# Router tail and first expert pass of a hybrid decoder layer: a second signal for the selection copy, a root split between two engines, and another order of membership and logits

## The reference, cut to what matters

```
x = x + einsum('bsc,cd->bsd', mixed, w_out)              # output projection
h = rms_norm(x, norm_ffn_g)
g_prob   = softmax(h @ w_rg + b_rg);  g_top, g_idx = top_k(g_prob, 1)     # 4 groups
e_logits = (h @ w_re + b_re)[group g_idx]                                # 8 experts in each
e_prob   = softmax(e_logits);  e_top, e_idx = top_k(e_prob, 2)
combine  = one_hot(g_idx*8 + e_idx) * (e_top / sum(e_top) * g_top)
act = silu(h @ w_gate[e]) * (h @ w_up[e]) * combine[e]     # 32 experts, 256 wide
x = x + sum_e act @ w_down[e]
return rms_norm(x, norm_final_g)
```

## Time and profile before

| | |
|---|---|
| median of 3 runs | 364.67 us (364.49 to 366.02) |
| the profiled execution | 363.79 us, of which its span is 361.6 us |
| PE busy | 312.5 us, 86% |
| DVE busy | 163.9 us, 45% |
| ACT busy | 125.0 us, 35% |
| POOL busy | 42.7 us, 12% |
| DMA | 121.17 MB, mean 335 GB/s |

### The profile page before, as it was taken

How to read it: one execution, slowest core, us unless ns; L and a number is a source line. 1 busy time by engine, 2 the same in 40 slices (tenths; PEclk the granted TensorE clock), 3 DMA queues, 4 the chain that set the end, 5 groups by cost and what they waited for, 6 DMA issues and landing times.

```text
span 361.6 us, 11575 instructions
## 1 busy us (share of the span) xinstructions
PE 312.5 (86%) x4740; PEld 240.3 (66%) x4741; DVE 163.9 (45%) x453; ACT 125.0 (35%) x307; POOL 42.7 (12%) x73
## 2 busy tenths in 40 slices
PE   1799999999999989889979898889999999766571
PEld 1699989889875545667657665657677777546250
DVE  2635545383353612774535344435555544341334
ACT  4726336545241426533313232312323323220223
POOL 1200000363402225620000000000000000000002
PEclk9899999999999999999989999999999999998997
DMA  8999795062729989489999999999999999999943
GB/s 254 352 386 387 263 392 239 3 237 112 280 81 400 314 353 387 160 304 348 418 414 357 418 418 414 416 418 410 423 412 421 418 415 423 410 424 416 414 175 116
DMA packets 32652, 121.17 MB, mean 335 GB/s; under 512 B 5497, under 2 KB 7825, under 8 KB 24689
## 3 DMA queue, kind: packets, MB, share of 16 engines
q1 hardware_dynamic: 32480, 120.65, 85.1%
q10 hardware_dynamic: 144, 0.13, 0.1%
HBM read 119.72 MB, written 1.05 MB: 334 GB/s over the span
## 4 chain that ended last, share of the span: by engine, by line
PE 68%; issue 8%; DMA 7%; DVE 4%; DVEq 4%; SPq 4%; ACT 3%; POOL 0%; POOLq 0%; ACTq 0%
PE bank L494 13%; PE bank L770 8%; PE bank L738 7%; PE bank L698 7%; PE bank L561 7%; PE bank L488 7%; DMA spare<-in_w_up_dram 6%; PE bank L705 4%; SPq L360 2%; PE bank L508 2%; PE bank L759 2%; ACT yb L1016 2%; PE bank L523 1%; DVEq L1431 1%; DMA ring<-in_norm_ffn_g_dram 1%
## 5 line engine op out<-in xcount | busy, mean ns | idle before, releaser
L738 PE MATMUL bank<-ring,hT 128*32 128x128 f32 x1664 | 53.2, 279 | 12.7 <-issue 4.7
L738 PEld LDWEIGHTS bank<-ring,hT 128*32 128x32 f32 x1664 | 46.1, 112 | 23.8 <-issue 23.3
L1426 DVE SCALAR_TENSOR_TENSOR yb<-bank,pp,yb 64x512 fp32r<-64x512 f32 x36 | 27.0, 749 | 45.8 <-ACT yb L1016 45.2
L1173 DVE TENSOR_TENSOR unit_lo<-ring,unit_hi 128x2048 fp32r<-128x2048 f32 (+1 forms) x12 | 26.3, 2207 | 32.6 <-ACT unit_hi L839 32.6
L698 PE MATMUL bank<-pp,qk 128*128 128x64 bf16 x912 | 30.6, 194 | 8.2 <-issue 4.7
L698 PEld LDWEIGHTS bank<-pp,qk 128*128 128x128 bf16 x912 | 28.1, 98 | 13.4 <-issue 7.4
L1016 ACT ACTIVATE yb<-bank,pp 64x512 fp32r<-64x512 f32 x36 | 24.6, 683 | 28.9 <-PE bank L770 28.4
L1078 POOL TENSOR_TENSOR stats<-stats 128x1 f32<-128x1 f32 (+1 forms) x7 | 4.6, 664 | 219.8 <-DVE stats L1457 199.7
L561 PE MATMUL bank<-ring,qk 128*128 128x512 f32 (+1 forms) x72 | 29.9, 551 | 0.0
L770 PE MATMUL bank<-ring,pp 128*32 128x512 f32 x208 | 25.0, 598 | 0.0
L705 PE MATMUL bank<-yb,selT 128*128 128x512 f32 x76 | 23.3, 428 | 1.7 <-DVE yb L1426 1.6
(11 more groups left out here) (197 smaller groups left out, 513.6 us busy)
## 6 DMA issues: line engine op xcount, KB each, us to landing
ring<-in_w_up_dram SPq DMA_DIRECT2D x24, 1024.0 KB, 19.1
ring<-in_w_down_dram SPq DMA_DIRECT2D x24, 1024.0 KB, 19.1
ring<-in_w_gate_dram SPq DMA_DIRECT2D x22, 1024.0 KB, 16.9
ring<-in_w_in_dram SPq DMA_DIRECT2D x5, 2048.0 KB, 19.4
ring<-in_w_out_dram SPq DMA_DIRECT2D x4, 1024.0 KB, 8.5
spare<-in_w_gate_dram SPq DMA_DIRECT2D x4, 1024.0 KB, 19.0
spare<-in_w_up_dram SPq DMA_DIRECT2D x4, 1024.0 KB, 19.7
work<-in_w_gate_dram SPq DMA_DIRECT2D x4, 1024.0 KB, 16.8
```

The source lines that it names most:

```text
L738: last = mm(p_gu[b:b + CAP, w * P:(w + 1) * P], hg[:, k, CAP * e:CAP * (e + 1)], w_gu[at[e]][:, w, k, h, :], start=(k == 0), stop=(k == KD ...
L1173: V.tensor_tensor(unit_lo[b][:, k, :], unit_src(u)[:, k, :], unit_hi[b][:, k, :].bitcast(fp32), ALU.subtract).then_inc(w_lo_ready, 1)
L1426: V.scalar_tensor_tensor(out=yb[half][rest, :], in0=p_y[rows, :], scalar=wcol[rows, :], in1=yb[half][rows, :].bitcast(fp32), op0=ALU.mult, ...
```

## The change

Five edits, all in the router's tail and in the signals of a pass:

1. PE: the four logit products of chunk 1 stood ahead of the last output projection. They now stand behind it, two ahead of the last chunk's transposes and two behind them, and `router_logits(3)` is behind those too.
2. DVE: `members(0)` stood right behind `best_two(0)`. It now stands behind the copy of chunk 3, the second tile's `mean_square` and the last `add_projection`.
3. ACT squares with a scale of 1/32, so its sums are already divided by 1024. `mean_square` is one DVE instruction in place of two for either tile. For tile 1 it adds the first two of three sums and no longer waits for the last chunk's.
4. POOL: `last_power` adds the last chunk's sum and then raises to -0.5, in place of `power(5, ...)`.
5. DVE makes the selection copy in `copy_selection` with a semaphore of its own, `selo_ready`; ahead of the first pass it stands ahead of the two `gain` instructions. PE waits for `selo_ready` ahead of the root products and for `selw_ready` only ahead of the transposed selection.

```diff
@@ tensor
+            def router_logits(n, k0=0, k1=KD):
-                for k in blocks(n):
+                for k in blocks(n)[k0:k1]:
...
             router_logits(2)
-            router_logits(1)
             out_proj(G_OM + LAST, 0, 2)
             transpose_x(3)
             out_proj(G_OM + LAST, 2, 4)
+            router_logits(1, 0, 2)
+            transpose_x(LAST)
+            router_logits(1, 2, 4)
             router_logits(3)
-            transpose_x(LAST)
             router_logits(LAST)
...
                         pe.wait_ge(selT_ready, i + 1)
-                        pe.wait_ge(selw_ready, i + 1)
+                        pe.wait_ge(selo_ready, i + 1)
                         for t in range(NT):
                             picked = mm(p_tr[:, 3 * P + 1:3 * P + 4], selo[:, t, :], rst[:, t, :], start=(t == 0), stop=(t == NT - 1))
...
                 pe.wait_ge(rrow_ready, i + 1)
+                pe.wait_ge(selw_ready, i + 1)
                 for t in range(NT):
                     mm(p_tr[:, t * P:(t + 1) * P], selo[:, t, :], identb, start=True, stop=True)
@@ scalar
-                ins = A(rest_of[n], x_chunk(n), ACT.Square, accum_out=sq5[:, SQ_AT[n]:SQ_AT[n] + 1])
-                if n in (2, LAST):
+                ins = A(rest_of[n], x_chunk(n), ACT.Square, scale=D ** -0.5, accum_out=sq5[:, SQ_AT[n]:SQ_AT[n] + 1])
+                if n >= 2:
                     ins.then_inc(ssq_ready, 1)
@@ gpsimd
+            def last_power():
+                pool.wait_ge(var_ready, 6)
+                pool.wait_ge(ssq_ready, 5)
+                step(nc.gpsimd.tensor_tensor(var[:, 1:2], var[:, 1:2], sq5[:, 4:5], ALU.add))
+                nc.gpsimd.tensor_tensor(rstdf[:, 1:2], var[:, 1:2], mhalf[:, 1:2], ALU.pow).then_inc(pow_ready, 1)
...
-            power(5, rstdf, 1, 1)
+            last_power()
@@ vector
                 dve.wait_ge(ssq_ready, 3 + t)
-                if t == 0:
-                    step(V.tensor_tensor(var[:, c], sq5[:, 0:1], sq5[:, 1:2], ALU.add))
-                else:
-                    step(V.scalar_tensor_tensor(out=var[:, c], in0=sq5[:, 2:3], scalar=sq5[:, 3:4], in1=sq5[:, 4:5],
-                                                op0=ALU.add, op1=ALU.add))
-                V.tensor_scalar(var[:, c], var[:, c], 1.0 / D, EPS, ALU.mult, ALU.add).then_inc(var_ready, 1)
+                V.tensor_scalar(var[:, c], sq5[:, 2 * t:2 * t + 1], sq5[:, 2 * t + 1:2 * t + 2], EPS, ALU.add, ALU.add).then_inc(var_ready, 1)
...
             best_two(0)
+            take_xT(3)
+            mean_square(1)
+            add_projection(G_OM + LAST)
             members(0)
-            take_xT(3)
-            add_projection(G_OM + LAST)
             take_xT(LAST)
-            mean_square(1)
...
+            def copy_selection(passes_before):
+                dve.wait_ge(sel_ready, passes_before + 1)
+                V.tensor_copy(selo.rearrange("p t (h c) -> p t h c", h=2),
+                              selb.unsqueeze(2).to_broadcast([P, NT, 2, CP])).then_inc(selo_ready, 1)
...
+            copy_selection(0)
             dve.wait_ge(gathered_half, 1)
             gain(0, p_hg).then_inc(hg_half_ready, 1)
...
-            weigh(0, 0)
+            weigh(0)
...
                 dve.wait_ge(actt_done, i + 1)
-                weigh(at_next, i + 1)
+                copy_selection(i + 1)
+                weigh(at_next)
```

More of the change, by code:

```diff
@@ L290, in layer_program @@
         r1_dve_ready, lo_dve_ready = sem("r1_dve_ready"), sem("lo_dve_ready")
-        hg_half_ready, gathered_half = sem("hg_half_ready"), sem("gathered_half")
+        hg_half_ready, gathered_half, selo_ready = sem("hg_half_ready"), sem("gathered_half"), sem("selo_ready")
         gate_half_done, gate_done = sem("gate_half_done"), sem("gate_done")
@@ L643, in transpose_x @@
                 last.then_inc(x2t_done, 1)
-            def router_logits(n):
+            def router_logits(n, k0=0, k1=KD):
                 t = CHUNKS[n][0]
@@ L1387, in _, with weigh @@
             step(V.tensor_tensor(wgt[:, :, 0:E], chosen[:, :, 0], chosen[:, :, 1], ALU.add))
-            def weigh(at_e, passes_before):
-                dve.wait_ge(sel_ready, passes_before + 1)
-                V.tensor_copy(selo.rearrange("p t (h c) -> p t h c", h=2), selb.unsqueeze(2).to_broadcast([P, NT, 2, CP]))
+            def weigh(at_e):
                 for t in range(NT):
@@ L1453, in _ @@
             own(2)
-            dve.wait_ge(ssq_ready, 5)
+            dve.wait_ge(ssq_ready, 6)
             V.tensor_tensor(ssq, ssq4[:, :, 0], ssq4[:, :, 1], ALU.add).then_inc(dve_step, 1)
```

## The result

| | before | after |
|---|---|---|
| median of 12 runs | 364.23 us (362.77 to 366.02) | 362.12 us (359.95 to 366.44) |
| profiled execution, its span | 363.79, 361.6 us | 362.38, 360.4 us |
| last up weights landed | 343.72 | 340.98 |
| from there to the end | 17.9 us | 19.4 us |

The ratio is 0.9941 (95% interval 0.9917 to 0.9965): 2.1 us faster, where 1.4 was forecast (363.3 us). In the profiled pair the span is 1.2 us shorter.

A forecast was written before the change was run, and what follows sets the result against it. The unbroken weight stream bounds the kernel, fed by PE's progress up to 193 us. Router's tail 1.1 plus first pass 0.3 gives 1.4 us, so 363.3 us against the median of 364.67; range 361.8 to 365.2.

The forecast's parts named there:

- What bounds: Whole kernel: time is the unbroken weight stream's start, plus its bytes at 417 GB/s, plus 17.9 us.
- Router's tail: From the last add to expert 6's down weights: ranks, selection, gather and those weights come 1.1 us earlier, bounds 0.4 to 1.3.
- Between transposes and `start_acc`: PE in the router's tail: six products plus transposes not overlapped take 1.6 us, where 1.40 us passed before.
- the power: POOL, last chunk's root: starts about 151.3 behind a 0.20 us addition, takes 0.84 us, ends 152.15.
- The membership: DVE, router's tail: moving `members(0)` from ahead of chunk 3's copy lets the last add start at 149.9 instead of 150.96.
- Copy beside POOL not stretched: DVE's copy of chunk 3 stays at 0.41 us beside POOL; if stretched, 1.1 us and a gain of 0.4.
- Move of PE's products: PE's logit products behind the last output projection: buys DVE almost nothing, expert 5's gate weights are issued at 149.0.
- First pass: Root products lose a 0.93 us wait, but the gather starts only 0.3 us earlier; bounds 0 to 0.93.
- Rival A: Third pass's 2.42 us PE stall changes; without it the 192 to 195 hole vanishes, 1.3 us more, 362.0 us; chance 0.16.
- the hole at 192 to 195: DMA falls to 232 GB/s, waiting for PE's fourth pass; lacks 1.3 us of transfers, forecast to get 0.3 shorter.
- The tail of 17.9 us: From the last up weights' landing to the end (last pass, final norm, stores): 17.9 us, untouched by the change.
- the forecast's own signs of being wrong: Stall near 182 of another length, chunk 3's copy over 0.5 us, or last weights not moving as PE did at 193.

The follow-up runs named there:

- experiment 4: Changed kernel with `members(0)` back right behind `best_two(0)`, ahead of the copy of chunk 3: 367.80 us, ratio 1.0094 to the kernel before.
- experiment 9: Changed kernel, equal instruction count, four 512-column products replacing the last k-block of up products in couples 5, 9 and 13: 363.48 us, ratio 0.9972 to the kernel before.
- experiment 12: Changed kernel without the scaled squares, shorter mean square and `last_power`: 363.79 us, ratio 0.9996 to the kernel before.
- experiment 11: Changed kernel with `members(0)` in its old place and two 512-column identity products ahead of the last transposes: 363.71 us, ratio 0.9989 to the kernel before.
- experiment 3: Changed kernel with PE's old order of logit products and last transposes: 363.25 us, ratio 0.9969 to the kernel before.
- experiment 1: Kernel before plus only the selection copy's own signal `selo_ready`: 364.99 us, ratio 1.0019 to the kernel before.
- experiment 2: Changed kernel without the selection copy's own signal, the router edits staying: 362.77 us, ratio 0.9966 to the kernel before.
- late_delay: Changed kernel with twenty extra 128-column identity products on PE in each of couples 5, 9 and 13: 382.35 us, ratio 1.0491 to the kernel before.
- experiments 9 and 10: The second: changed kernel, equal instruction count, four 384-column products replacing the last up k-block in couples 7, 11 and 15: 364.19 us, ratio 0.9963 to the kernel before.
- experiments 6 to 8: Changed kernel with extra 128-column products: 14 each in couples 7, 11, 15; 20 in the second pass; 20 each in couples 5, 9, 13: 387.46, 382.78, 382.35 us.
- experiment 5: Changed kernel with `members(0)` in its old place and eight 128x128 identity products ahead of the last transposes: 369.1 us, ratio 1.0144 to the kernel before.

## Why the prediction came out right

- **What bounds** (stream start, 417 GB/s, then the tail): held. Stretches of 146 and 148.5 us run at the same 417 GB/s; experiment 4 moves the start late and the end late, and experiment 9 adds 10.5 us of PE work behind 195 for nothing measurable, within the 13.1 us that PE waited for weights there.
- **Router's tail, 1.1 us**: right, a little low at the ranks. Net of the 0.33 the last add gained 1.1 (forecast 1.06), `start_acc` 1.05 (0.85), `best_two(1)` 1.5 (1.3), the ranks 1.34 (1.1), expert 6's down weights 1.35 (1.1). Two terms were mis-sized. Between transposes and `start_acc` 1.53 us pass, not 1.6; the power costs 0.56 and not 0.84, and only with the last root as in the kernel before (experiment 12) is it 0.84 again. Why the same operation has two durations, no run shows. The trace before had both, and the forecast took the longer: the first tile's power took 0.55 there, also behind two VectorE steps:

```profile
146.22 0.55 POOL L1078 TENSOR_TENSOR stats<-stats 128x1 f32<-128x1 f32 x1 [1.32 <-DVE stats L1294]
```

- **The membership is the term that pays**: experiment 11 puts it at 1.1 to 1.2 us in the trace. That its old place, with the new order of products, can cost 5.6 us, through a clock that falls behind the wait that the two make together, was in no case of mine.
- **Copy beside POOL not stretched, 0.41**: right, 0.42. The moved membership is also cheaper: L1318 0.37 and L1320 0.19, where L1312 took 0.60.
- **Move of PE's products, nothing**: right; experiment 3, by its trace and within its interval.
- **First pass, 0.3 us**: the gather comes net 1.62 earlier, 0.28 beyond the ranks. As a time it is below what the runs can tell (experiments 1 and 2).
- **Rival A**, given 0.16, showed its effect in this pair. The stall stayed but the clock behind it did not fall, the hole at 192 to 195 went, and the landing moved 2.74 us: 0.33 upstream, 1.35 with the down weights, 1.06 from the hole, near the 1.3 worked out for it; the gather's 0.28 is in this 1.06. It was not the stall's vanishing: 2.02 us remain. Nor does the moved stall account for the clock: in experiment 2 it stands in its old place and the clock stays at 1.00, and of the fourteen traces only those of the kernel before and of late_delay have a low clock at 184 to 188 us. So this 1.06 us is likelier an accident of the profiled execution before than a gain of the change.
- **The tail of 17.9 us "that the change doesn't touch"** is the step that was wrong. It was 19.4, by the clock behind the last wait: the up products took 1.4 us more and the gather 0.2. So 0.33 upstream, 1.35 of the router's tail and 1.06 of the hole, less 1.5 here, make the span's 1.2.
- **Luck has a part in it.** Two of the forecast's own signs of being wrong came true: the stall has another length (2.02 for 2.42), and the last weights moved by 2.74 us where SP's load at 193 moved by 3.6. In the profiled pair a gain of 1.06 that the forecast had left to rival A and a loss of 1.5 that it had at nothing nearly cancel.

So the forecast's steps are shown in one trace each, and a gain of 1 to 2 us in the medians. Other variants that by their edits should take within 0.3 us of the changed kernel's time (experiments 2, 3 and 9) had ratios of 0.9966 to 0.9972, just above the upper end of its interval; the changed kernel was not timed again beside them, so my estimate of its worth is 1.0 to 2.1 us, and the forecast's 1.4 lies in it. A low clock in one of three places costs 1.5 to 1.7 us where a trace has it, as much as the effect: in the router's tail (`start_acc` 4.52 us for 2.82), behind the third pass's stall (4.7 for 3.1), behind the last wait (5.1 for 3.5, up products and gather). That executions of one kernel differ in which of them they meet is argued, since there is one trace of each; the twelve executions of the changed kernel have mean granted clocks from 0.961 to 0.983.

## What to carry to other kernels

Where weights stream without a break, count only what moves the start of the stream, and then look at how long TensorE stands in front of it: here 1.1 us of VectorE work in the wrong place cost 5.6 us once PE had no products left to put into the wait, and 3.8 of them came back with the wait filled. Ask that too of an engine's wait that a change lengthens, and not only of what it delays. When an experiment adds instructions to an engine whose loop is long, keep the number of instructions equal, by wider ones in place of others: three of mine measured stalls at the jump back for the most part. Look for the stall even then, as experiments 9 and 10 had it at equal length.

## What the runs showed of the hardware

- **The jump back of a long TensorE loop can cost 6.5 to 7.8 us.** With 21 or 22 instruction packets on the page neither jump back shows such a stall, with 30 or 31 one, with 40 two: nine or ten packets each. With 56 or 80 more instructions in the program (experiments 6 to 8) both came, with 32 more one (experiment 5), with 8 more none (experiment 11); but at the changed kernel's own length experiments 9 and 10 had one each, and so had experiment 1, which executes one instruction less. What decides at equal length stays open. The Trainium skill, "Runtime: NRT & Kernel Launch", section "Instruction fetch mechanics", says that a taken branch to a block that isn't loaded waits for its fetch. The traces agree in that the stall stands at the jump back and comes with more instruction packets; the rows here give the cost.
- **Straight code stalls too**: 1.1 to 2.5 us, at places that shift with the number of instructions ahead of them. The one that the earlier trace rows shows at 184.59 ahead of the gather stands one product earlier in the changed kernel, whose passes have one wait more, and ahead of the gather again in experiment 2, whose passes don't.
- **TensorE's clock after a wait is not a matter of that wait's length alone.** Behind the last wait of 2.9 us the same 64 products took 1.95 us before, 3.33 after, and 3.00, 2.61, 3.61, 3.21 and 3.30 in experiments 2, 3, 4, 11 and 12. The wait for the gate weights ahead of them doesn't decide it either: it was 1.55 us before and 1.59 in experiment 12. Behind the wait of 2.06 us in experiment 4 the granted clock was near 0.57 for eight microseconds; behind 0.97 us, in the same place of the changed kernel, it stayed at 1.00, and behind 0.98 us in experiment 2 it was 0.58 over four.
